# Latent attention on one core: the products with the values issued one step later

## The reference, cut to what matters

```python
MLA_HEADS = 8; QK_NOPE_DIM = 64; QK_ROPE_DIM = 32; V_HEAD_DIM = 64; Q_BLOCK = 128

def block(args):                      # one block of 128 queries
    qn_b, qr_b = args
    s = (jnp.einsum("bqhd,bkhd->bhqk", qn_b, k_nope)
         + jnp.einsum("bqhd,bkd->bhqk", qr_b, k_rope))
    p = jax.nn.softmax(s.astype(jnp.float32) * scale, axis=-1).astype(v.dtype)
    return jnp.einsum("bhqk,bkhd->bqhd", p, v)
o = lax.map(block, (qn, qr))          # four blocks of queries
```

## Time and profile before

| what | value |
|---|---|
| runs | 2577.68, 2569.20, 2566.73 us |
| median | 2569.2 us |
| the profiled execution's own time | 2579.75 us |
| its span, first to last instruction | 2577.9 us |
| stage mla on PE, within the span | from 1729.81 us to some 1818 us |

### The profile page before, as it was taken

How to read it: one execution, slowest core, us unless ns; L and a number is a source line. 1 busy time by engine, 2 the same in 40 slices (tenths; PEclk the granted TensorE clock), 3 DMA queues, 4 the chain that set the end, 5 groups by cost and what they waited for, 6 DMA issues and landing times. The chain is left out here.

```text
span 2577.9 us, 33670 instructions
## 1 busy us (share of the span) xinstructions
PE 2387.9 (93%) x13722; PEld 1720.0 (67%) x13722; DVE 1211.0 (47%) x1806; ACT 831.6 (32%) x1281; POOL 33.4 (1%) x57
## 2 busy tenths in 40 slices
PE   6998889999999989799899999997998989999997
PEld 4873668888888866577688888874797643333322
DVE  3698445552455342475564465655553332322224
ACT  5110553321233232276443244355454311001001
POOL 0000000000000001100000000000000000000000
PEclk8999989999999989899899999998999989999998
DMA  5249311121112124200223223210241469999995
GB/s 238 69 150 310 123 41 66 57 79 53 58 65 70 62 108 186 102 2 34 87 94 113 82 101 103 86 59 1 82 148 33 172 271 421 421 421 421 421 421 234
DMA packets 75779, 390.83 MB, mean 152 GB/s; under 512 B 9088, under 2 KB 13440, under 8 KB 44800
## 3 DMA queue, kind: packets, MB, share of 16 engines
q1 hardware_dynamic: 75648, 388.97, 40.1%
HBM read 380.22 MB, written 2.10 MB: 148 GB/s over the span
## 5 line engine op out<-in xcount | busy, mean ns | idle before, releaser
L264 DVE TENSOR_TENSOR WLO<-RAW,WHI 128x1024 fp32r<-128x1024 f32 (+3 forms) x226 | 279.2, 1236 | 727.4 <-ACT WHI L253 727.3
L282 PE MATMUL PS<-XNH,WHI 128*128 128x512 f32 (+1 forms) x1888 | 594.4, 359 | 15.5 <-DVE WLO L264 4.7
L282 PE MATMUL PS<-XNL,WHI 128*128 128x512 f32 (+1 forms) x1888 | 590.1, 357 | 0.0
L282 PE MATMUL PS<-XNH,WLO 128*128 128x512 f32 (+1 forms) x1888 | 588.4, 356 | 0.0
L253 ACT ACTIVATE WHI<-RAW 128x1024 fp32r<-128x1024 f32 (+3 forms) x226 | 241.5, 1069 | 820.9 <-PE PS L282 802.5
L282 PEld LDWEIGHTS PS<-XNH,WHI 128*128 128x128 f32 x1888 | 319.5, 189 | 77.9 <-issue 14.7
L282 PEld LDWEIGHTS PS<-XNH,WLO 128*128 128x128 f32 x1888 | 321.2, 189 | 54.2
L282 PEld LDWEIGHTS PS<-XNL,WHI 128*128 128x128 f32 x1888 | 319.8, 189 | 53.0 <-issue 2.4
L2781 PE MATMUL PS<-RAWM,XS 128*64 128x512 f32 x1016 | 239.3, 601 | 17.2 <-DMA RAWM<-experts 16.2
L2781 PEld LDWEIGHTS PS<-RAWM,XS 128*64 128x64 f32 x1016 | 65.6, 136 | 155.2 <-issue 88.8
L282 PE MATMUL PS<-HL,WHI 128*128 128x512 f32 (+1 forms) x528 | 160.8, 359 | 0.0
(11 more groups left out here) (353 smaller groups left out, 2545.8 us busy)
## 6 DMA issues: line engine op xcount, KB each, us to landing
RAWM<-experts SPq DMA_DIRECT2D x191, 1024.0 KB, 17.3
RAW<-up SPq DMA_DIRECT2D x88, 512.0 KB, 3.2
ADAW<-ada SPq DMA_DIRECT2D x40, 1024.0 KB, 10.3
RAW<-down SPq DMA_DIRECT2D x32, 704.0 KB, 4.0
RAW<-pw SPq DMA_DIRECT2D x24, 512.0 KB, 3.5
ADAL<-ada SPq DMA_DIRECT2D x8, 1024.0 KB, 6.9
V<-V SPq DMA_DIRECT2D x64, 101.0 KB, 3.5
RAW<-qkv SPq DMA_DIRECT2D x12, 512.0 KB, 3.3
```

Source lines behind the costliest of these rows:

```text
L264: dve.tensor_tensor(prog.WLO[:, at % SPLITS, 0:to.length], prog.RAW[:, at % RAWS, 0:to.length], f32(prog.WHI[:, at % SPLITS, 0:to.length]) ...
L282: last = pe.matmul(prog.PS[:, to, a:b], w, x[:, k, a:b], start=(k == 0 and n == 0), stop=(k == g.k - 1 and n == 2))
```

## The change

On PE, values(n-1) is issued behind transposes(n) and ahead of scores(n+2), where values(n) stood behind scores(n+2); values(7) follows behind the loop. On ACT, the copies of the full `outs` of a group move with them: `keep_hi(0)` stands behind copies(4) and ahead of exponentials(6) (it stood behind exponentials(5) and ahead of copies(4)); `keep_hi(1)` stands behind the loop. DVE's order is unchanged, and no instruction is added or removed.

```diff
@@ PE
             for n in range(STEPS):
                 transposes(n)
+                if n >= 1:
+                    values(n - 1)
                 if n + 2 < STEPS:
                     scores(n + 2)
-                values(n)
+            values(STEPS - 1)
@@ ACT
             exponentials(1)
+            def keep_hi(g):
+                for pair in range(2):
+                    p = 2 * g + pair
+                    act.wait_ge(attended, p + 1)
+                    act.activation(prog.XNH[:, 4 + p, 0:LAT], outs[pair], ACT.Copy).then_inc(out_hi, 1)
             for n in range(STEPS):
                 copies(n)
+                if n % NB == 0 and n > 0:
+                    keep_hi(n // NB - 1)
                 if n + 2 < STEPS:
                     exponentials(n + 2)
-                if n % NB == NB - 1:
-                    for pair in range(2):
-                        p = 2 * (n // NB) + pair
-                        act.wait_ge(attended, p + 1)
-                        act.activation(prog.XNH[:, 4 + p, 0:LAT], outs[pair], ACT.Copy).then_inc(out_hi, 1)
+            keep_hi(STEPS // NB - 1)
```

## The result

| | before | after |
|---|---|---|
| median (11 runs each) | 2569.2 us | 2592.38 us |
| lowest to highest | 2565.62 to 2584.59 us | 2578.53 to 2595.06 us |
| ratio after / before | | 1.0065, 95% interval 1.0048 to 1.0081 |
| profiled execution's own time | 2579.75 us | 2578.53 us |

What follows compares the result with a forecast made beforehand. The prediction took a loop through PE, DVE and ACT, 8.41 us a round with no engine full, to bound the attention stage. Its terms, 11.4 − 5.7 + 7.7 = +13.4 us, gave 2582.6 us, range 2573 to 2591.

Steps and rivals of the forecast that it cites:

- The loop and the six values: Attention stage: six values, 1.90 us each, enter the loop ahead of scores; regular rounds 8.41 to 10.31 us, +11.4 us.
- The place between the groups: Rounds of 9.38 and 13.18 us become regular as waits around emptying the output tiles go: −0.97 and −4.77, together −5.7 us.
- The clock: PE gaps of 3.3 us in six rounds: three falls to half clock of six, 2.55 us each, +7.7 us.
- The sum: Whole kernel: 11.4 − 5.7 + 7.7 = +13.4 us, giving 2582.6 us against 2569.2, slower by 0.52%.
- the change adds the same wherever a run lies: Whole kernel: +13.4 us, derived on the profiled execution of 2579.75 us, was added to the median 2569.2 us.
- rival 1: PE's longer gaps: clock holds, no fall or one; +5.7 to +8.2 us, taken at 2574.9 us; chance 0.25.
- Rival 2: PE's longer gaps: clock falls in five or six; +18.4 to +21.0 us, taken at 2590.2 us; chance 0.21.
- Rival 3: Attention loop: values ahead of scores fill idle PE time, only −5.7 us is left, 2563.5 us; chance 0.04.
- Rival 4: PE's queue might still begin the scores early, so the change does nothing; 2569.2 us; chance 0.02.

Runs made afterwards that it cites:

- in_gap: Against after: values(n-1) moved between the second and third head of transposes(n), the rest unchanged; 0.9983 (0.9965 to 1.0001) against before.
- before_twice: Against before: values(1), values(2) and values(5) issued twice in their old place behind scores; profiled execution 2589.53 us, no ratio given.
- filled: Against after: values issued a second time between the second and third head of the next transposes, in five of six gaps; 1.0034 (1.0015 to 1.0053) against before.
- few_values: Against after: products with the values left out for steps 0, 1, 2, 4 and 5; profiled execution 2586.16 us, no ratio given.
- after_again: The kernel after, unchanged, run again for a second trace; 1.0050 (1.0032 to 1.0068) against before, profiled execution 2594.06 us.

## Why the prediction was right or wrong

*The loop and the six values (+11.4)*: right. 8.41 + 1.90 = 10.31 was forecast, 10.30 measured (the 1811.62 us that the prediction gives for values(6) is the row of the transposes behind them; they start at 1809.72, and nothing hangs on it); `in_gap`, `before_twice` and `filled` show from three sides that work in the hole is free and work ahead of scores is not.

*The place between the groups (−5.7)*: right for the trace it was made against, where both long rounds became regular, and too large for the kernel in general. The 13.18 us contained a fall which two other traces of before lack (10.64 and 10.65). Over three traces the refund is 0.97 and a mean of 3.1, together −4.1. The prediction took a term of one execution for one of the kernel.

*The clock (+7.7: three falls at 2.55)*: the count was right, three and then twice four, though the prediction had no row that decided it and took the middle of its bounds; some of that is luck. (Its two nearest rows are not equally near either: 3.21 lies 0.1 us under the gap and 3.52 lies 0.2 over.) The price was the mis-sized term: some 1.5 us a fall, 4.7 for the three. The passages at half clock that the price was taken from lasted 6.8 us. Behind the gaps of 3.28 us every one of the eleven in the three traces of after lasted 3.4 (one in `few_values` lasted 6.8). Busy time in these passages, the two of before and then the three of after:

```profile
1748.64:1755.47 6.83, 5.59 (x17) 2.77 (x17) 1.75 (x7) 2.77 (x6) 0.00 (x0) 0.50 0.01 2
1793.02:1799.84 6.82, 5.43 (x40) 4.85 (x40) 4.16 (x14) 2.46 (x7) 0.00 (x0) 0.50 0.00 0
```

```profile
1752.63:1756.04 3.41, 3.41 (x30) 2.94 (x28) 0.00 (x0) 0.26 (x1) 0.00 (x0) 0.50 0.00 0
1762.87:1766.28 3.41, 3.22 (x22) 2.92 (x24) 0.78 (x3) 1.72 (x4) 0.00 (x0) 0.50 0.02 5
1807.24:1810.66 3.42, 3.42 (x31) 3.09 (x28) 0.00 (x0) 0.24 (x1) 0.00 (x0) 0.50 0.02 5
```

PE worked 5.4 to 5.6 us at half clock there and 3.2 to 3.4 here. Half of that is a rough estimate of what is lost: 2.7 or 2.8 us against 1.6 or 1.7. Where the fall begins matters less: the second of after began inside its gap (the transposes behind it took 1.94 us), the first and the third after it, at nearly the same price. Why the passages are shorter is not shown. A fall that begins after the restart, in `after_again`, takes the first transposes at the full-clock 1.11 us, then the values at 3.39 for 1.97, and the scores at 2.19 for 1.99:

```profile
1762.37 1.11 PE L2078 MATMUL PS<-IDENT,T 128*128 128x128 f32 x8 [3.28 <-ACT PT L2164]
1763.40 3.39 PE L2092 MATMUL PS<-PT,VT 128*64 128x128 f32 x32
1766.72 2.19 PE L2055 MATMUL PS<-KN,QN 64*128 64x512 f32 x8
```

*The sum*: against the trace of before, 11.4 − 5.7 + 4.7 = 10.4, and the stage shows 10.25; +13.4 was forecast. Against the mean of three traces, 11.4 − 4.1 + 5.5 (3.7 falls at 1.5) = 12.8, and the stages show 12.9. The error in the price and the one in the refund nearly cancel, so that +13.4 comes so near the 12.9 is luck: it stands on a wrong pair of terms.

*Against the median*: the step "the change adds the same wherever a run lies" holds for the stage, not for the medians. By the ratio the kernel after is at 2585.9 us, 3.3 over the forecast; by its median it is 9.8 over. The median of before lies in the lower group of its runs (2565.62 to 2572.57) and that of after in the upper group of its own. The two paces, some 10 us apart, would make 2592.38 of 2582.6, but this is not shown, as only profiled executions show their pace.

*The rivals*: rival 1 (the clock holds) is out by three traces. Rival 2 (every gap) is out too: 11 of 18 gaps of 3.28 us were followed by a fall. The "HAM oscillation" section of "TensorE: Matmul & The Clock Gate" in the Trainium skill has the fall in every iteration, but of a loop that waits some 3 to 5 us for DMA each time. The prediction left that out and read the page as speaking of any wait; so its gaps of 1.39 us were no test of the page, and the 3.28 us here lie at the short end of those waits. That a loop with such a gap pays for the clock again and again, though not each time, the traces bear out. Rival 3 (values hidden) failed on DVE's idle time as said, 5.39 us now. Rival 4 (the scores begin early) is out by the timeline of after, where the values stand ahead of L2055.

## What to carry to other kernels

Before moving an engine's work within its order, write the round as a chain of starts and ask whether the work lies in the chain or beside it; here 1.90 us of matmuls moved from a hole of 3.3 us into the chain, though every instruction and wait stayed the same. If a hole exists, ask which queue made it: two copies queued behind four exponentials on ACT made this one, and taking them forward was worth more than any place for the values. And take a price from more than one execution where the clock is part of it.

## What the runs showed of the hardware

- The same gap can end at full or at half clock: 3.21 us fell in one trace of before and not in two, 2.35 us fell in `before_twice` and in no trace of before, and in `in_gap` the clock fell in the tail behind gaps of 1.39 and 0.30 us. The length of a gap alone does not decide.
- A gapless stretch of matmuls at a granted clock of 1.00 runs at one of two paces in different executions of one kernel, 69.33 or 70.67 us for 400 matmuls in the first ffn. It makes some 10 us of this kernel's time, nearly as much as the change: the stage began at 1719.8 to 1722.2 us in the four traces with 69.33 and at 1729.0 to 1736.2 in the nine with 70.67. No profile here shows its cause.
